# Interleaved weight panels at eight transitions of a float32 two-block model, and two more split buffers in its second layer

## What is computed

```
for l in range(DEPTH):
    h = rms_norm(x, pre_norm[l])
    ...
    y = jnp.concatenate([(y_br * jax.nn.silu(gate.astype(jnp.float32))).astype(x.dtype),
                         y_mem * jax.nn.silu(g_mem)], axis=-1) @ w_out[l]
    x = x + rms_norm(y, post_norm[l])
```

```
h = h + 0.5 * swiglu(rmsnorm(h, ffn1_norm[l]), ffn1_w_gate[l], ffn1_w_up[l], ffn1_w_down[l])
h = h + hybrid_mixer(rmsnorm(h, mix_norm[l]), pos, k_top, w_in[l], w_ret_out[l], w_att_out[l], w_mix_out[l])
h = h + 0.5 * swiglu(rmsnorm(h, ffn2_norm[l]), ffn2_w_gate[l], ffn2_w_up[l], ffn2_w_down[l])
```

## Time and profile before

| | us |
|---|---|
| median of 3 runs | 1318.83 |
| lowest, highest | 1318.52, 1320.29 |
| the profiled execution's own time | 1320.18 |
| its span in the trace | 1318.4 |
| PE busy in the span | 1213.6 (92%) |
| DVE busy | 845.1 (64%) |
| ACT busy | 631.4 (48%) |
| POOL busy | 198.6 (15%) |

### The profile page before, as it was taken

One profiled execution on the slowest core, in us unless ns is written; L12 is line 12 of the kernel. 1 busy time (PEld: TensorE's weight loads), 2 busy tenths in 40 slices (PEclk: granted clock), 3 DMA queues, 4 the chain that ended last, 5 costly groups with the idle time before them and its releaser, 6 DMA issues.

```text
span 1318.4 us, 23948 instructions
## 1 busy us (share of the span) xinstructions
PE 1213.6 (92%) x9724; PEld 1163.2 (88%) x9724; DVE 845.1 (64%) x1452; ACT 631.4 (48%) x1081; POOL 198.6 (15%) x194
## 2 busy tenths in 40 slices
PE   6987879787997899999999999989999999999997
PEld 6976768587896899999999998889999999999997
DVE  5767954555665676665478764769656667877642
ACT  5766343444455564443344343653345445644442
POOL 2125320220001212120022100005100001122101
PEclk9989868988999989999999999999999999999999
DMA  6432310031442365555355542235545445755560
GB/s 251 150 109 96 97 64 1 33 128 65 158 131 96 128 237 180 175 166 173 120 160 160 170 157 91 97 112 176 173 168 170 130 143 178 235 183 188 159 196 32
DMA packets 53533, 185.78 MB, mean 141 GB/s; under 512 B 6704, under 2 KB 8880, under 8 KB 53168
## 3 DMA queue, kind: packets, MB, share of 16 engines
q1 hardware_dynamic: 52720, 180.97, 42.3%
q10 hardware_dynamic: 704, 3.29, 0.7%
HBM read 183.19 MB, written 1.05 MB: 140 GB/s over the span
## 4 chain that ended last, share of the span: by engine, by line
PE 72%; DVE 14%; ACT 9%; issue 3%; POOL 1%; DMA 1%; DVEq 0%; ACTq 0%; POOLq 0%
PE bank L2433 20%; PE bank L2436 20%; PE bank L2434 20%; DVE wl L1889 3%; ACT wh L1516 2%; PE bank L2448 1%; ACT L1493 1%; DVE zl L1981 1%; DVE sqr L1985 1%; PE bank L2568 1%; PE bank L2457 1%; ACT scb L1762 1%; DMA cols<-vecs 1%; DVE tmp L2346 1%; DVE tmp L2344 1%
## 5 line engine op out<-in xcount | busy, mean ns | idle before, releaser
L2433 PE MATMUL bank<-xh,wh 128*128 128x256 f32 (+1 forms) x2008 | 585.8, 292 | 21.1 <-DVE xl L2130 11.1
L2436 PE MATMUL bank<-xh,wl 128*128 128x256 f32 (+1 forms) x2008 | 575.9, 287 | 6.6 <-DVE wl L1889 6.5
L2434 PE MATMUL bank<-xl,wh 128*128 128x256 f32 (+1 forms) x2008 | 576.6, 287 | 0.0
L1889 DVE TENSOR_TENSOR wl<-raw,wh 128x1024 fp32r<-128x1024 f32 (+1 forms) x343 | 422.7, 1238 | 233.9 <-ACT wh L1516 232.4
L1516 ACT ACTIVATE wh<-raw 128x1024 fp32r<-128x1024 f32 (+1 forms) x343 | 356.1, 1044 | 309.4 <-PE bank L2436 297.7
L2433 PEld LDWEIGHTS bank<-xh,wh 128*128 128x128 f32 x2008 | 384.7, 192 | 30.7 <-issue 21.8
L2436 PEld LDWEIGHTS bank<-xh,wl 128*128 128x128 f32 x2008 | 386.4, 192 | 8.0 <-DVE wl L1889 8.0
L2434 PEld LDWEIGHTS bank<-xl,wh 128*128 128x128 f32 x2008 | 385.4, 192 | 0.6
L2433 PE MATMUL bank<-hh,wh 128*128 128x272 f32 (+1 forms) x352 | 100.3, 285 | 0.0
L2434 PE MATMUL bank<-hl,wh 128*128 128x272 f32 (+1 forms) x352 | 100.2, 285 | 0.0
L2436 PE MATMUL bank<-hh,wl 128*128 128x272 f32 (+1 forms) x352 | 100.2, 285 | 0.0
(11 more groups left out here) (362 smaller groups left out, 1568.1 us busy)
## 6 DMA issues: line engine op xcount, KB each, us to landing
raw<-w_ffn_gate SPq DMA_DIRECT2D x44, 512.0 KB, 3.6
raw<-w_ffn_up SPq DMA_DIRECT2D x44, 512.0 KB, 3.7
raw<-w_a_w_in SPq DMA_DIRECT2D x29, 512.0 KB, 3.5
raw<-w_ffn_down SPq DMA_DIRECT2D x32, 448.0 KB, 3.4
raw<-w_w_out SPq DMA_DIRECT2D x16, 512.0 KB, 3.5
raw<-w_b_w_in SPq DMA_DIRECT2D x16, 512.0 KB, 4.4
raw<-w_ffn_down SPq DMA_DIRECT2D x16, 512.0 KB, 3.6
raw<-w_ret SPq DMA_DIRECT2D x16, 512.0 KB, 3.5
```

Of the source, the lines that this page charges most:

```text
L1889: v.tensor_tensor(lo[:, c], raws[n % N_RAW][:, c], hi[:, c].bitcast(F32), ALU.subtract).then_inc(*w_lo.up(n))
L2433: pe.matmul(ps, hi[:, c], x_hi(k), start=(k == 0), stop=False)
L2434: pe.matmul(ps, hi[:, c], x_lo(k), start=False, stop=False)
L2436: last = pe.matmul(ps, lo[:, c], x_hi(k), start=False, stop=(k == kt - 1))
```

## The change

1. **Groups.** `begin(items, part)` takes a bank and a weight entry for each of two or three panels and issues one step `mm_group`; `finish` issues the tiles that are left, gives the split buffers back and puts the evacuations off. On PE the step goes tile by tile, and at each tile through all panels of the group. Before its first matmul it waits for the high part of every panel in it.
2. **Where.** Two panels: `w_out0` (tiles 6 and 7, the memory half, before the first group norm is summed, the others behind the norms), `w_out1` (tiles 0 to 5, then the last step of the memory heads, then tiles 6 and 7), `idx` 5 and 4 at the mixer's start, `mix_out` 0 and 1. Three panels: `b_w_in` 0, 1, 2 at the start of layer 1 (1 and 2 leave `LAYER1_BETWEEN`), gate 0, up 0, gate 1 at the start of ffn1 and of ffn2. The sum of squares stands behind the group.
3. **Split buffers.** `N_EXTRA1` = 2 more (`wh0_0`, `wh0_1`) from the end of `w_out0` up to the fifth panel of `w_out1`. `weights` now issues a split only where a buffer is free.
4. **Branch.** `branch0` and `branch` become steps per pair and per tile; the memory half of layer 0 is split before the group norms.
5. **Small.** The step `lam` (four vectors, two columns on PE, an exponential on ACT) moves from the start of layer 1 to the start of the program. Memory heads of layer 1 have 4 buffers `mpt1` for 2.

```diff
-N_EXTRA = 4
+N_EXTRA, N_EXTRA1 = 4, 2
...
-LAYER1_BETWEEN = [pair for h in range(1, BT) for pair in (("b_w_in", h), ("w_kv", h), ("w_kv", BT + h - 1))] \
+LAYER1_BETWEEN = [pair for h in range(1, BT) for pair in (("b_w_in", h), ("w_kv", h), ("w_kv", BT + h - 1))
+                  if pair not in (("b_w_in", 1), ("b_w_in", 2))] \
...
-    order += [("b_w_in", 0, KT), ("w_kv", 0, KT)]
+    order += [("b_w_in", p, KT) for p in range(3)] + [("w_kv", 0, KT)]
...
-                    while len(n_hi) < min(len(ready) + 1 + lag, n + depth[0], len(STREAM)):
+                    while len(n_hi) < min(len(ready) + 1 + lag, n + depth[0], len(STREAM)) and split_ring.free:
                         split_hi()
+                    if len(n_hi) == len(ready):
+                        break
                     split_lo()
...
+            def begin(items, part=range(KT)):
+
+                group, given = [], []
+                for name, panel, src, n_tok, evac in items:
+                    b, freed = bank.take()
+                    n, buf = weights(name, panel, 0)
+                    last_chunk[name, panel] = n
+                    group.append((n, buf, b, freed, src, n_tok))
+                    given.append((evac, panel, b, n))
+                do("mm_group", group, part, True, len(part) == KT)
+                return group, given, len(part) == KT, [k for k in range(KT) if k not in part]
+
+            def finish(begun):
+                group, given, done, rest = begun
+                if not done:
+                    do("mm_group", group, rest, False, True)
+                for n, buf, *_ in group:
+                    give_split(buf, n)
+                settle(last=False)
+                late.extend(given)
...
+            do("branch0", 3)
+            da0 = norm_a(0)
+            begun = begin_out(0, (6, 7))
+            norm_b(0, da0)
+            da1 = norm_a(1)
+            norm_b(1, da1)
+            da2 = norm_a(2)
+            do("branch0", 0)
+            norm_b(2, da2)
+            do("branch0", 1)
+            do("branch0", 2)
+            mix_out(0, begun)
+            more_splits(N_SPLIT, N_EXTRA1)
             do("phase", 0)
...
-            project("b_w_in", [0], "pre1", S, q_evac, hook=lambda: stat("pre1"), keep=True)
+            finish(begin([("b_w_in", p, "pre1", S, q_evac) for p in range(3)]))
+            stat("pre1")
             do("kv_split")
             project("w_kv", [0], "kvn", S, k_evac)
-            b, freed = bank.take()
-            do("lam", b, freed)
-            bank.give(b, (lam_e, 0))
...
+            for i in range(BT):
+                do("branch", i)
+            begun = begin_out(1, range(BT))
+            for g in memory_ends:
                 for _ in g:
                     pass
-
-            skewed([diff_head(h) for h in range(BT)] + [memory_stream(j) for j in range(MT)])
-            do("branch")
-            mix_out(1)
+            do("branch", BT)
+            do("branch", BT + 1)
+            mix_out(1, begun)
...
+                finish(begin([(f"ffn{n}_gate", 0, f"ffn{n}", FFN_TOK[n], gate_evac),
+                              (f"ffn{n}_up", 0, f"ffn{n}", FFN_TOK[n], up_evac),
+                              (f"ffn{n}_gate", 1, f"ffn{n}", FFN_TOK[n], gate_evac)]))
+                stat(f"ffn{n}")
...
-            project("idx", [5], "mixq", S, idx_evac, hook=mix_stat, keep=True)
-            project("idx", [4], "mix", T, idx_evac, keep=True)
+            finish(begin([("idx", 5, "mixq", S, idx_evac), ("idx", 4, "mix", T, idx_evac)]))
+            mix_stat()
...
-            project("mix_out", list(range(KT)), "mg", S, mix_evac)
+            finish(begin([("mix_out", p, "mg", S, mix_evac) for p in range(2)]))
+            project("mix_out", list(range(2, KT)), "mg", S, mix_evac)
...
+                elif kind == "mm_group":
+                    group, part, first, last_part = a
+                    for n, buf, b, freed, src, n_tok in group:
+                        if first:
+                            on.wait_ge(*w_hi.past(n))
+                            after(on, freed)
+                    for k in part:
+                        for n, buf, b, freed, src, n_tok in group:
+                            hi, lo = splits[buf]
+                            x_hi, x_lo, ready, tag = SRC[src]
+                            ps, c = banks[b][:, 0:n_tok], slice(k * P, (k + 1) * P)
+                            on.wait_ge(*ready.past((tag, k // 2 if tag == "y0" else k)))
+                            pe.matmul(ps, hi[:, c], x_hi(k), start=(first and k == part[0]), stop=False)
+                            pe.matmul(ps, hi[:, c], x_lo(k), start=False, stop=False)
+                            on.wait_ge(*w_lo.past(n))
+                            end = last_part and k == part[-1]
+                            last = pe.matmul(ps, lo[:, c], x_hi(k), start=False, stop=end)
+                            if end:
+                                last.then_inc(*used.up(n))
```

More of the change, by code:

```diff
@@ L360, in build @@
         mp1 = [sb(f"mp1{i}", [P, 2, MEM], ph) for i in range(4)]
-        mpt1 = [sb(f"mpt1{i}", [P, 2, S], ph) for i in range(2)]
+        mpt1 = [sb(f"mpt1{i}", [P, 2, S], ph) for i in range(4)]
         mst1 = [sb(f"mst1{i}", [P, 16], ph) for i in range(2)]
@@ L365, in build @@
         stb = [sb(f"stb{i}", [P, 16], ph) for i in range(4)]
+        splits += [(sb(f"wh0_{i}", [P, WC], ph, F32R), sb(f"wl0_{i}", [P, WC], ph, F32R)) for i in range(N_EXTRA1)]
         ph.close()
@@ L588, in weights, with more_splits @@
                 while len(ready) < min(n + depth[0] - lag, len(STREAM)):
-                    while len(n_hi) < min(len(ready) + 1 + lag, n + depth[0], len(STREAM)):
+                    while len(n_hi) < min(len(ready) + 1 + lag, n + depth[0], len(STREAM)) and split_ring.free:
                         split_hi()
+                    if len(n_hi) == len(ready):
+                        break
                     split_lo()
-                if len(n_hi) < n + depth[0]:
+                if len(n_hi) < n + depth[0] and split_ring.free:
                     split_hi()
                 return n, ready[n]
-            def more_splits(base):
-                extra.extend(range(base, base + N_EXTRA))
-                depth[0] += N_EXTRA
-                for b in range(base, base + N_EXTRA):
-                    split_ring.give(b)
+            def more_splits(base, n, *events):
+                extra.extend(range(base, base + n))
+                depth[0] += n
+                for b in range(base, base + n):
+                    split_ring.give(b, *events)
             def fewer_splits():
-                split_ring.free = [f for f in split_ring.free if f[0] not in extra]
+                for f in [f for f in split_ring.free if f[0] in extra]:
+                    split_ring.free.remove(f)
+                    extra.remove(f[0])
                 depth[0] = N_SPLIT
@@ L731, in memory_heads, with out_evac, begin_out, mix_out @@
                 bank.give(b, (ym, (layer, j)))
-            def mix_out(layer):
-                sbank, freed = bank.take()
-                tag, n_sum = f"mo{layer}", SUMMED[f"mo{layer}"]
+            def out_evac(layer):
                 def evac(panel, b, n):
                     do("mo_evac", layer, panel, b, n)
-                    add_square(tag, panel)
+                    add_square(f"mo{layer}", panel)
                     return ((mo_y, (layer, panel)),)
-                for panel in range(KT):
-                    project(f"w_out{layer}", [panel], f"y{layer}", S, evac, keep=True)
+                return evac
+            def begin_out(layer, part):
+                return begin([(f"w_out{layer}", panel, f"y{layer}", S, out_evac(layer)) for panel in range(2)], part)
+            def mix_out(layer, begun):
+                sbank, freed = bank.take()
+                n_sum = SUMMED[f"mo{layer}"]
+                finish(begun)
+                for panel in range(2, KT):
+                    if layer == 1 and panel == KT - 3:
+                        fewer_splits()
+                    project(f"w_out{layer}", [panel], f"y{layer}", S, out_evac(layer), keep=True)
                 do("mo_stat", layer, n_sum - 1, sbank, freed)
@@ L776, in schedule @@
             do("x_norm")
+            b, freed = bank.take()
+            do("lam", b, freed)
+            bank.give(b, (lam_e, 0))
             project("w_mem0", [3], "mem0", MEM, v_evac, keep=True)
+            do("lam_use")
             k_evac, v_evac, done1 = memory_kv(1)
@@ L986, in group_norm @@
                 bank.give(da, (gn_w, j))
-            skewed(group_norm(j) for j in range(3))
-            do("branch0")
-            mix_out(0)
+            do("branch0", 3)
[11 more added lines that the diff above has]
+            more_splits(N_SPLIT, N_EXTRA1)
             do("phase", 0)
@@ L1119, in ffn @@
                 do("phase", f"ffn{n}", last_chunk[f"ffn{n}_down", KT - 1])
+            assert not extra
             ffn(1)
```

(8 more changed lines are left out.)

61 lines of the change are left out of this document (29 added, 32 removed).

## The result

The changed kernel takes 1335.22 us (median of 4 runs, 1333.35 to 1335.80), the kernel before 1319.56 (4 runs, 1318.52 to 1321.25): ratio 1.0115, 95% interval 1.0097 to 1.0133, slower by 1.2%. The forecast was 1331, the range 1324 to 1338. The profiled execution has a span of 1333.3 us, 14.9 more than before.

A forecast was written before the change was run, and what follows sets the result against it. PE, busy 92% of the span, was taken as the bound, losing time to waits and slow-clock spells. The terms summed to +11.9 us: 1332.1 against the profiled execution, 1330.7 against the median, stated as 1331 us, range 1324 to 1338.

The forecast's parts named there:

- Start of layer 1, +5.4: Layer 1's first group: PE waits for the third panel's late high part, starting at 299.98 instead of 291.95; net +5.4 us.
- ffn1, +6.2: Start of ffn1: same wait for the group's weights, start at 468.8, then a slow spell of 25 matmuls; +6.2 us.
- ffn2, +5.2: Start of ffn2: a new gap of 3.3 us before the group, with a slow spell behind it; +5.2 us, without it +3.0.
- End of layer 0, -3.0: Twelve memory-half matmuls fill the gap between group norms, though the norm chain ends later; -3.0 us, ends -4.1 and -1.7.
- Heads, -0.9: Layer 1's heads: extra buffers remove 2.5 us of `wl` waits, later first scores cost 1.6; -0.9 us, ends -3.6 and +2.
- End of the heads, +0.3: End of layer 1's heads: `w_out1` starts earlier but waits for tiles 6 and 7; +0.3 us, ends -1 and +1.5.
- Mixer's start, -0.4: The `idx` pair's gain, less a low part split behind the rope tables' scaling; -0.4 us, ends -1.3 and +0.5.
- `mix_out`, -0.9: The pair at `mix_out`: the stall of 0.86 us before the last tile at 1097.40 goes; -0.9 us.
- The rest of the mixer, 0: Mixer between its start and `mix_out`: the prediction gave no term, so no change.
- Rival 1: Group starts: third weight not late because split before the `xh` copies; about -10 us, 1309 us; chance 0.04.
- Rival 2: Whole kernel: gains in layer 0, heads and tail at their upper ends; about +1, 1320 us; chance 0.09.
- Rival 3: Group matmuls: changing bank each time runs them at the slow clock; +27, 1358 us; chance 0.05.

The follow-up runs named there:

- run 1: The change with its groups of three made groups of two, the third panel alone behind the sum of squares: 1307.14 us, 0.9912 of the kernel before.
- run 2: The change, groups of three kept, with the two extra split buffers handed out earlier, ahead of panel 6 of `w_out0`: 1324.77 us, 1.0044 of the kernel before.
- run 6: The kernel before with only the change's end of layer 0 (and the code it needs): 1311.76 us, 0.9948 of the kernel before.
- run 5: The change with its three groups of three undone and without the two extra split buffers: 1316.51 us, 0.9976; with those buffers 1313.36 us.
- run 10: run 7 with the end of layer 1's heads and `w_out1` as in the kernel before: 1302.83 us, 0.9877 of the kernel before.
- run 7: run 1 with the mixer's first pair undone (`idx` 5, sum of squares, `idx` 4, as before): 1304.14 us, 0.9881 of the kernel before.

## Why the prediction was right, point by point

The mechanism was right at the three starts, which make the sign and most of the size. That the total came within 4 us of 1331 is in part luck: terms missed upwards (the mixer) and downwards (heads, layer 0) cancelled in part, and so did errors within ffn1 and ffn2.

- **Start of layer 1, +5.4: right, +6.1.** The group started at 296.66. By run 1's wait of 4.28 us its first `xl` was there at 283.98 + 4.28 = 288.3, 8.4 us earlier; I had 299.98 - 291.95 = 8.0. The 72 matmuls took 11.2 us, to the sum of squares at 307.84; I had 11.0. Run 2 shows the cause. The releaser, the length of the wait (12.68 and 13.30, I had "about 12") and, here, the clock in the first third (26 of 72 matmuls) are as listed.
- **ffn1, +6.2: right, +6.1**, by two errors that nearly cancel. The group started 13.30 us behind the norm's sum, I had 468.8 - 455.99 = 12.8; and the slow spell had 15 matmuls, where I had 25, about 1 us less.
- **ffn2, +5.2: right in its mechanism, +4.5.** The gap was 3.88 us, I had 3.3 (+0.6), and the spell had 14 matmuls, not 26 (-1.2). The clock did fall, which I had chosen between two ends, and that choice was luck. The trace of before already had two waits of 3.23 us of PE, before 86.89 and before 107.76; behind the one the clock is 0.50, behind the other 1.00:

```profile
86.90:89.90 3.00, 3.00 (x12) 2.82 (x13) 1.56 (x2) 1.38 (x2) 0.73 (x1) 0.50 0.00 0
107.80:110.80 3.00, 3.00 (x24) 2.95 (x25) 1.56 (x2) 1.37 (x3) 0.74 (x1) 1.00 0.00 0
```

  So waits of this length don't fix the outcome. The Trainium skill (TensorE: Matmul & The Clock Gate, section "HAM oscillation — how this bites in real kernels") tells of a kernel whose every burst starts slowly behind a wait. The burst at ffn2 did, at 0.50; the second of the two waits above shows that not every one does. I had quoted the section without its condition on the wait's length, so it should not have decided the term.
- **End of layer 0, -3.0: right on average.** It is two values, -2.3 and -4.2 (run 6); my ends were -1.7 and -4.1, and the reason was the one that I gave.
- **Heads, -0.9: under-sized, -3.1.** I took 2.5 us of waits for `wl` and charged 1.6 for later first scores. The waits went (run 5 puts 2.9 to 3.2 us on the buffers). The 1.6 was the mis-sized part. The wait for `kT` did grow, from 0.7 to 3.59 us, but the later ones for `scb` (2.5 to 1.4) and `small` (1.8 to none in the heads) shrank with it. PE's idle time in the stretch went from 9.7 to 7.4, that is 2.3 less; the other 0.8 is busy time beyond the moved panels and is not explained.
- **End of the heads, +0.3: right in its sign, +0.9** (run 10: 0.8).
- **Mixer's start, -0.4: wrong sign, +1.7.** I named the low part that is split behind the rope tables and priced it at half a microsecond; it is 0.98, and two more waits follow, of 0.41 and 0.87 (run 7).
- **`mix_out`, -0.9: right, -1.1.**
- **The rest of the mixer, 0: missed, +3.6.** Here the prediction had no term. Some 1.9 us are the spell at 877, 1.5 the one at 1080, in unchanged code; 0.2 are spread.
- The sum was +11.9 and the trace has +14.9. The mixer's two misses make +5.7, the heads -2.2, layer 0 with what lies ahead of it -0.7, the end of the heads +0.6, all others together -0.3. The forecast was low by what it missed in the mixer, not by the starts.
- **Rivals.** Rival 1 is what run 2 makes of layer 1's start; in the change its condition (ACT splits the third weight ahead of the copies) is not met. Rival 2's heads did reach about its 3 us, but the starts did not reach their ends. Rival 3 is out by the clock row of 1135.2 to 1143.3; the rule named there (same page of the Trainium skill, "A second HAM failure mode: psum-queue depth-cycling") is not seen here.

## What to carry to other kernels

A group that begins together begins when its last operand is ready. Count the buffers first: with three split buffers two panels were ready ahead of the norm, the third was not, and it turned a gain of 2 us at the starts of layer 1 and ffn1 into a loss of 6, and at ffn2 one of under 1 us into a loss of 4.5. When a wait stands in front of a group, ask for each member what it is queued behind on the engine that makes it. Take such a change apart before judging it: of its eight places three cost 17 us at their starts and 22 in all, two more cost 2.5 together in their own stretches, and with pairs in place of the threes and those two undone it runs in 1303 us, where the kernel before takes 1319.

## What the runs showed of the hardware that was not expected

- The same wait of 2.9 us in the same instructions leaves TensorE's clock at 1.00 in one program and drops it to 0.54 in another, the same way in two executions of each. All six kernels with the `idx` pair had a slow spell there, of the six without it two. So the pair is not the whole reason. The change paid some 2 us for it, 170 us behind its nearest edit. Why the clock falls there is not settled. Nor does the length of a wait fix it elsewhere: of two waits of 3.23 us in one trace, one was followed by 0.50 and one by 1.00.
- Where twelve matmuls came into a gap of 4.3 us the clock mostly stayed up, though not every time. Both traces of the kernel before fall to 0.50 behind that gap at layer 0's end; of twelve traces with the new end eight stayed at 1.00 and four fell, and the one kernel that was traced twice did each once. The difference is 1.9 us, about as much as the spread between executions of one kernel.
